# First head's first eight experts ahead of the rest, TensorE's order around them, and small moves at the start and in the gates, in a two-block transformer kernel on one core

## The reference

```python
for l in range(DEPTH):                       # 2
    h = rmsnorm(x, norm_mix_g[l])
    x = x + mixer_block(h, ...)              # mLSTM with 4 heads, windowed attention with 16 heads, gated
    h = rmsnorm(x, norm_mlp_g[l])
    x = x + sqrelu_mlp(h, w_up[l], w_down[l])
x = rmsnorm(x, final_norm_g)
```

```python
y = sum over heads and their 16 experts of
        softmax(best sums)[e] * gelu(x . expert_u[e]) * expert_v[e]
```

## Time and profile before

| | us |
|---|---|
| median of 3 runs | 1753.12 |
| lowest and highest | 1752.78, 1753.4 |
| the profiled execution's own time | 1752.94 |
| its span, first to last instruction | 1751.2 |

### The profile page before, as it was taken

One profiled execution on the slowest core, in us unless ns is written; L12 is line 12 of the kernel. 1 busy time (PEld: TensorE's weight loads), 2 busy tenths in 40 slices (PEclk: granted clock), 3 DMA queues, 4 the chain that ended last, 5 costly groups with the idle time before them and its releaser, 6 DMA issues.

```text
span 1751.2 us, 21314 instructions
## 1 busy us (share of the span) xinstructions
PE 1613.2 (92%) x8160; PEld 1183.5 (68%) x8160; DVE 1159.2 (66%) x2030; ACT 835.1 (48%) x1555; POOL 379.0 (22%) x374
## 2 busy tenths in 40 slices
PE   7999999999999999999999999799987788778786
PEld 6998998888898899888889998455522232222232
DVE  5757865666665776566675556788676767767654
ACT  4456635333455664533355545454444444444443
POOL 0100001000120000100050102565543444334440
PEclk9999999999999999999999999999999999999999
DMA  7444454555544355455544365999999999999996
GB/s 293 161 144 145 152 209 155 198 185 187 198 166 140 125 183 214 168 193 192 186 151 145 145 217 194 414 421 421 422 421 421 422 421 422 422 421 422 421 421 270
DMA packets 67206, 464.43 MB, mean 265 GB/s; under 512 B 7457, under 2 KB 9633, under 8 KB 11809
## 3 DMA queue, kind: packets, MB, share of 16 engines
q0 software_dynamic: 36864, 268.45, 36.9%
q1 hardware_dynamic: 29952, 194.29, 30.8%
q10 hardware_dynamic: 288, 0.33, 0.1%
HBM read 462.00 MB, written 1.05 MB: 264 GB/s over the span
## 4 chain that ended last, share of the span: by engine, by line
PE 65%; DMA 21%; DVE 6%; issue 4%; ACT 3%; POOL 0%; SPq 0%; POOLq 0%; ACTq 0%
PE acc L579 13%; PE acc L581 13%; PE acc L580 13%; DMA arena<-in_peer_uv,arena 10%; DMA row_w_lo<-in_peer_uv,arena 5%; PE att L604 5%; DMA row_w_hi<-in_peer_uv,arena 4%; PE acc L1718 4%; PE acc L1721 4%; PE acc L604 3%; PE att L605 3%; PE acc L605 1%; DVE w_lo L553 1%; DVE arena L2132 1%; PE att L904 1%
## 5 line engine op out<-in xcount | busy, mean ns | idle before, releaser
L553 DVE TENSOR_TENSOR w_lo<-arena,w_hi 128x2048 fp32r<-128x2048 f32 x171 | 391.7, 2300 | 172.8 <-ACT w_hi L546 172.5
L546 ACT CAST w_hi<-arena 128x2048 fp32r<-128x2048 f32 x175 | 333.6, 1907 | 121.8 <-PE acc L581 100.2
L1840 ACT ACTIVATE arena<-arena 128x1 f32<-128x1 f32 x256 | 51.9, 203 | 322.7 <-DVE arena L2132 139.5
L2132 DVE SCALAR_TENSOR_TENSOR arena<-arena 128x1024 f32<-128x1024 f32 x114 | 139.3, 1223 | 84.9 <-DMA arena<-in_peer_uv,arena 83.1
L579 PE MATMUL acc<-xa,w_hi 128*128 128x256 f32 x672 | 192.9, 287 | 0.0
L580 PE MATMUL acc<-xa,w_lo 128*128 128x256 f32 x672 | 190.8, 284 | 0.0
L581 PE MATMUL acc<-xa,w_hi 128*128 128x256 f32 x672 | 190.7, 284 | 0.0
L1718 PE MATMUL acc<-arena,gate_raw 128*128 128x512 f32 x226 | 128.1, 650 | 46.8 <-ACT gate_raw L1850 46.3
L2326 POOL DMA_INDIRECT arena<-in_peer_uv,arena x114 | 129.6, 1137 | 151.4 <-PE acc L1721 141.1
L604 PE MATMUL att<-xa,w_hi 128*128 128x512 f32 x384 | 136.0, 398 | 0.0
L579 PEld LDWEIGHTS acc<-xa,w_hi 128*128 128x128 f32 x672 | 129.2, 192 | 3.6 <-issue 3.0
(11 more groups left out here) (309 smaller groups left out, 3545.7 us busy)
## 6 DMA issues: line engine op xcount, KB each, us to landing
arena<-in_units SPq DMA_DIRECT2D x175, 1024.0 KB, 4.8
arena<-in_bias SPq DMA_DIRECT2D x1, 2048.0 KB, 9.3
arena<-in_peer_uv,arena POOLq DMA_INDIRECT x114
x_res<-in_x SPq DMA_DIRECT2D x2, 512.0 KB, 6.5
arena<-in_norm_mix_g SPq DMA_DIRECT2D x2, 512.0 KB, 6.9
arena<-in_units SPq DMA_DIRECT2D x2, 512.0 KB, 8.1
arena<-in_norm_mlp_g SPq DMA_DIRECT2D x2, 512.0 KB, 6.6
arena<-in_norm_g SPq DMA_DIRECT2D x2, 512.0 KB, 5.8
```

The costliest lines, as they stand in the source:

```text
L546: nc.scalar.copy(w_hi[:, s, :], raw[HOME[g]]).then_inc(S["hi_ready"], 1)
L553: nc.vector.tensor_tensor(w_lo[:, s, :], raw[HOME[g]], w_hi[:, s, :].bitcast(F32), ALU.subtract).then_inc(S["lo_ready"], 1)
L2132: nc.vector.scalar_tensor_tensor(row, row, 1.0, hn[:, n // SLOTS, :], ALU.mult, ALU.mult, accum_out=dots[:, n:n + 1]).then_inc(S["rows_use ...
```

## The change

It has four parts. (1) `first_experts()` on VectorE, ahead of tile 1's split: it takes the 8 best of each half's scores, the 64 sums of these, the 8 best sums and their experts, and writes the first 8 indices; the 8 best sums of 16 x 16 lie among these 64. GpSimd waits for it ahead of item 0 and for the whole routing of head 0 ahead of item 8. `route(0, 0)` leaves out what is done. (2) The order around it: on TensorE the second half of tile 0's queries runs through ahead of tile 1's transposes, which are cut in two around `rank_half(1)`; on ScalarE `first_take(1)` goes ahead of tile 1's copies; in unit mix 3, tile 0's transposes come one step earlier; on VectorE tile 0 is split whole ahead of the last sum; on GpSimd the iota goes ahead of tile 1's norm. (3) At the start, the first norm's weights are loaded on ScalarE's queue; unit 1 is rounded in two halves, and its remainder made half by VectorE, behind the norm of tile 1, and half by GpSimd. (4) `gate_columns` runs for heads 0 and 1 in the middle of unit aq 0, for heads 2 and 3 behind it.

```diff
@@ start
-            sp.dma_start(g_next, rows_of(A["norm_mix_g"][0:1, :])).then_inc(S["g_loaded"], mark("g_loaded", "mix", 16))
+            act.dma_start(g_next, A["norm_mix_g"][0:1, :].broadcast_to([P, D])).then_inc(S["g_first_loaded"], 16)
+        def second_hi(act, half):
+            cols = slice(half * UNIT // 2, (half + 1) * UNIT // 2)
+            if half == 0:
+                act.wait_ge(S[f"w_loaded{HOME[1]}"], at(f"w_loaded{HOME[1]}", 1))
+            nc.scalar.copy(w_hi[:, SLOT[1], cols], raw[HOME[1]][:, cols]).then_inc(S["first_hi" if half == 0 else "hi_ready"], 1)
+        def second_lo(eng, op, half):
+            cols = slice(half * UNIT // 2, (half + 1) * UNIT // 2)
+            if half == 0:
+                eng.wait_ge(S["first_hi"], 2)
+            else:
+                eng.wait_ge(S["hi_ready"], 2)
+                eng.wait_ge(S["lo_ready"], 1)
+            op(w_lo[:, SLOT[1], cols], raw[HOME[1]][:, cols], w_hi[:, SLOT[1], cols].bitcast(F32), ALU.subtract).then_inc(
+                S["first_lo" if half == 0 else "lo_ready"], 1)
@@ layer_act, l == 0
                 norm_act(act, "mix", 1)
-                split_hi(act, 1)
+                second_hi(act, 0)
+                second_hi(act, 1)
@@ layer_dve, l == 0
-                split_lo(dve, 1)
                 norm_dve(dve, "mix", 1, g_next)
+                second_lo(dve, nc.vector.tensor_tensor, 0)
@@ layer_pool
             norm_pool(pool, "mix", 1)
+            if l == 0:
+                second_lo(pool, nc.gpsimd.tensor_tensor, 1)
@@ layer_pe
+                    elif (l, u) == (0, 1):
+                        pe.wait_ge(S["first_lo"], 2)
+                        pe.wait_ge(S["lo_ready"], 2)
-                    within = {("gb", 3): turn_hm, ("aq", 1): gate_more_columns}.get((name, i), lambda: None)
+                    within = {("gb", 3): turn_hm, ("aq", 0): lambda: gate_columns((0, 1)), ("aq", 1): gate_more_columns}.get((name, i), lambda: None)
...
                 elif (name, i) == ("aq", 0):
-                    gate_columns()
+                    gate_columns((2, 3))
@@ by_tile
-                        half_t(b, s, xh, xl, t, k0[n_], first[n_], last[n_], range(3))
+                        half_t(b, s, xh, xl, t, k0[n_], first[n_], last[n_], range(2))
+                        if n_ == 1:
+                            earlier(t)
+                        half_t(b, s, xh, xl, t, k0[n_], first[n_], last[n_], range(2, 3))
@@ first_queries
                 queries_of(0, 1, range(4))
                 rank_half(0)
-                tile_pe(pe, "n2", 1)
                 queries_of(0, 1, range(4, 8))
-                queries_of(1, 0, range(2))
+                tile_pe(pe, "n2", 1, range(4))
                 rank_half(1)
-                queries_of(1, 0, range(2, 8))
+                tile_pe(pe, "n2", 1, range(4, 8))
+                queries_of(1, 0, range(8))
                 queries_of(1, 1, range(8))
@@ second_pe, mix 2
-                            lambda t: tile_pe(pe, "n2", 0) if t == 1 else None)
+                            earlier=lambda t: tile_pe(pe, "n2", 0) if t == 1 else None)
@@ second_act
             first_rank(0)
+            first_take(1)
             tile_act(act, xb_hi, "n2", 1)
-            first_take(1)
             first_rank(1)
@@ second_dve
+            def first_experts():
+                for i in range(2):
+                    scores_ = rank[0][:, i, :]
+                    dve.wait_ge(S["rank_ready"], at("rank_ready", (0, 0, i)))
+                    nc.vector.max(top_s[:, i, 0:8], scores_)...
+                    nc.vector.max_index(top_i[:, i, 0:8], top_s[:, i, 0:8], scores_)...
...
+                nc.vector.tensor_copy(expert[:, 0:8], f_expert).then_inc(S["expert_ready"], mark("expert_ready", "first"))
@@ peer_norm
-                tile_dve(dve, xb_hi, xb_lo, "n2", 0, [0])
+                tile_dve(dve, xb_hi, xb_lo, "n2", 0)
                 unit("mix", 3)
                 mix_add(1, 1)
-                tile_dve(dve, xb_hi, xb_lo, "n2", 0, [1])
                 norm_dve(dve, "n2", 1, g_peer)
+                first_experts()
                 tile_dve(dve, xb_hi, xb_lo, "n2", 1)
@@ second_pool
-            for t in range(TT):
-                norm_pool(pool, "n2", t)
+            norm_pool(pool, "n2", 0)
             nc.gpsimd.iota(iota_i, pattern=[[1, P_TOP]], base=0, channel_multiplier=0).then_inc(S["iota"], mark("iota", 0))
             pool.wait_ge(S["iota"], at("iota", 0))
             nc.gpsimd.tensor_copy(iota16, iota_i).then_inc(S["iota"], mark("iota", 1))
+            norm_pool(pool, "n2", 1)
...
             for n in range(ITEMS):
-                if n % P_TOP == 0:
+                if n == 0:
+                    pool.wait_ge(S["expert_ready"], at("expert_ready", "first"))
+                elif n % P_TOP == 0 or n == 8:
```

More of the change, by code:

```diff
@@ L82 @@
     "first_hi": "the rounded part of half of the first unit", "first_lo": "and the rest of it",
+    "g_first_loaded": "the first norm's weights are here",
     "first_loaded": "half of the first unit is here", "x_loaded_too": "the second tile of tokens is here",
@@ L442, in build @@
         wsum = area("ak", 1280, ALL_HEADS)
+        f_top = area("ak", 1296, 16).rearrange("p (i k) -> p i k", i=2)
+        f_cand = area("ak", 1312, 64).rearrange("p (a b) -> p a b", a=8)
+        f_best, f_pos = area("ak", 1376, 8), area("ak", 1384, 8).bitcast(U32)
+        f_pos_i = area("ak", 1392, 16).bitcast(U32).rearrange("p (i k) -> p i k", i=2)
+        f_pos_f = area("ak", 1408, 16).rearrange("p (i k) -> p i k", i=2)
+        f_pick = area("ak", 1424, 128).rearrange("p (i k a) -> p i k a", i=2, k=8)
+        f_both = area("ak", 1552, 16).rearrange("p (i k) -> p i k", i=2)
+        f_expert = area("ak", 1568, 8)
         ROW = 2 * D
@@ L468, in unit_dma @@
                 sp.wait_ge(S["lo_ready"], LAST_AT_HOME[g] + 1)
+            if LAST_AT_HOME[g] == 1:
+                sp.wait_ge(S["first_lo"], 2)
             s = HOME[g]
@@ L637, in half_t, with by_tile @@
             return m
-        def by_tile(pe, operands, ua, k0, first, last, tag, between=lambda t: None, normed=None, in_halves=False):
+        def by_tile(pe, operands, ua, k0, first, last, tag, between=lambda t: None, normed=None, in_halves=False,
+                    earlier=lambda t: None):
             for t in range(TT):
@@ L701, in norm_dve, with tile_pe @@
                     S["hn_ready"], mark("hn_ready", (tag, t, b)))
-        def tile_pe(pe, tag, t):
-            for k in range(KT):
+        def tile_pe(pe, tag, t, ks=range(KT)):
+            for k in ks:
                 if k % 4 == 0:
@@ L829, in gate_products, with gate_columns @@
                 m.then_inc(S["gate_done"], mark("gate_done"))
-            def gate_columns():
+            def gate_columns(heads):
                 pe.wait_ge(S["gate_m"], at("gate_m"))
-                for h in range(M_HEADS):
+                for h in heads:
                     nc.tensor.matmul(att[h // 2][:, (h % 2) * SEQ:(h % 2 + 1) * SEQ], ident[0:M_HEADS, h:h + 1].broadcast_to([M_HEADS, P]), g_M,
@@ L1390, in layer_dve @@
             if l == 0:
-                dve.wait_ge(S["g_loaded"], at("g_loaded", "mix", "start"))
+                dve.wait_ge(S["g_first_loaded"], 16)
                 norm_dve(dve, "mix", 0, g_next)
@@ L2069, in route @@
                 if part == 0 and g == 0:
-                    dve.wait_ge(S["iota"], at("iota", 1))
-                    for i in range(2):
-                        dve.wait_ge(S["rank_ready"], at("rank_ready", (0, 0, i)))
-                        top_first(t, h, halves[i:i + 1])
+                    for values, val, idx, i in halves:
+                        dve.wait_ge(S["routed"], at("routed", ("first8_at", i)))
+                        nc.vector.match_replace(values, val[:, 0:8], values, LOWEST).then_inc(
+                            S["routed"], mark("routed", ("top8_out", (t, h, i))))
                 elif part == 0:
@@ L2110, in route @@
                     dve.wait_ge(S["routed"], at("routed", ("expert_f", (t, h))))
-                    c = t * SLOTS + h * P_TOP
-                    nc.vector.tensor_copy(expert[:, c:c + P_TOP], expert_f).then_inc(
+                    c, known_ = t * SLOTS + h * P_TOP, 8 if g == 0 else 0
+                    nc.vector.tensor_copy(expert[:, c + known_:c + P_TOP], expert_f[:, known_:P_TOP]).then_inc(
                         S["expert_ready"], mark("expert_ready", (t, h)))
```

36 lines of the change are left out of this document (added).

## The result

The changed kernel took 1768.55 us (median of four runs, 1767.04 to 1769.5), the kernel before 1752.95 beside it: a ratio of 1.0088, 95% interval 1.0075 to 1.0102, so 15.6 us slower. The forecast was +0.4. The profiled execution took 1769.1, its span 1767.3, 16.1 more than before.

The account below looks back on a forecast made before the run. TensorE was taken to bound the kernel until about 1100 us, then the gather's DMA stream at 421 to 422 GB/s. Terms +1.1 - 1.5 + 0.8 = +0.4 us on 1752.94 gave 1753.3, as median 1753.5; range 1750.2 to 1755.8.

Parts of the forecast that it names:

- the clock's term: Behind TensorE's hole ahead of tile 1's queries: 3.2 us of work at half speed, 1.6 us; bounds 0 and 3.3.
- the slacks: Delay the gather's items can take: item 7 5.5 us, item 18 2.4 plus 2.4 of TensorE waits; gone at 4.8.
- experts ahead: First experts and the order around them: 1.1 us slower; 0.5 faster without the clock's fall, 2.8 slower with the long one.
- columns in three: Gate columns in shorter pieces keep TensorE's clock up behind them: 1.5 us faster, bounds 0 and 1.5.
- start: Unit 1's halves 1.0 us slower, norm weights on ScalarE's queue 0.2 faster: 0.8 slower; bounds 0.4 faster, 1.0 slower.
- The sum of first_experts(): VectorE's steps behind the second half's scores: 3.7 us in all, first numbers at 1084.2 instead of 1089.4.
- The iota moved ahead ... Both nothing.: On GpSimd ahead of the second norm: query unit 1's remainder starts sooner, ending before anyone wants it; no effect.
- The hole: TensorE idle 5.0 us ahead of tile 1's queries, waiting for tile_dve queued behind first_experts() on VectorE.
- Rival four: The hole costs double: clock at 1.2 GHz for 6.7 us of work, item 18 2.8 us late, 1755.2; chance 0.12.
- Row 0: First gathered row used 5.9 us later: 4.3 from the order and 1.6 from the clock.
- the 0.8 that was free: Ahead of row 0: of TensorE's 5.1 us delay, 0.8 is free before VectorE's remainder of query unit 3 ends.
- Item 7's slack of 5.5: In the gather: landing at 1115.7, less 4.65 us, less its issue's end at 1105.6; 0.4 us late after 5.9.

Follow-up runs that it names:

- hole_filled: experts_norm_first with 39 discarded matmuls (13 steps of three, 128 columns) put into TensorE's hole ahead of tile 1's queries: 1757.99 us, 1.0027 of the kernel before.
- hole_filled_full: As hole_filled, with 16 discarded steps instead of 13, which leave no pause: 1754.75 us, 1.0011 of the kernel before.
- experts_split_ahead: As experts_norm_first, with tile 1's split ahead of first_experts() on VectorE: 1751.5 us, 0.9991 of the kernel before.
- start_halves_vector: The kernel before with only unit 1's remainder in two halves, both on VectorE and nothing on GpSimd: 1752.96 us, 1.0000 of the kernel before.
- experts_norm_first: The kernel before with the experts' part alone, but GpSimd's iota and cast back behind both norms: 1760.83 us, 1.0043 of the kernel before.

## Why the prediction was wrong

Four steps failed: that moving the iota costs nothing (3.0 us), the clock's term (6.2 for 1.6), the columns (+1.4 for -1.5) and the start (+2.4 for +0.8); and the slacks held less than the sum gave them (2.3 us more). For the experts this closes: 3.0 + 4.6 + 2.3 = 9.9, and 11.05 - 1.1 = 9.95.

| term | forecast | alone on the chip |
|---|---|---|
| experts ahead | +1.1 | +11.05 |
| columns in three | -1.5 | +1.4 |
| start | +0.8 | +2.4 |
| sum | +0.4 | +14.8 (the whole: +15.6) |

- **The sum of first_experts().** Right: 3.6 us from the second half's MAX8 to the end of the cast (1089.12 to 1092.69) against 3.7, and the first numbers at 1084.06 where nothing disturbs it (1084.2 forecast).
- **"The iota moved ahead ... Both nothing."** This step failed. I asked when the remainder of query unit 1 is wanted, and not what runs on VectorE when it starts. It is a GpSimd instruction with two SBUF operands beside a VectorE one, the very pair that the prediction priced at the start. It cost 3 us. The Trainium skill, "SBUF — State Buffer", section "SBUF: two separate sides", says that whichever of the two starts first holds the ports for its whole instruction and the other is blocked. The trace agrees: a lead of 0.07 us decided over 4.3 (5.68 against 1.41).
- **The hole.** Right in size (5.05 us against 5.0) and in cause (tile_dve queued behind first_experts()).
- **The clock behind it.** The mechanism was right, the term mis-sized: 1.6 forecast, bounds 0 to 3.3, and 6.2 measured. It failed where I read how long the clock stays low from the products of whole rows (3.2 us, from 1100.8 to 1104.0). In tile 1's queries it stayed at 0.5 for all their 48 products of 128 columns (in hole_filled from the 22nd on), and came back 2.1 to 2.4 us (4.3 in hole_filled) after the 256-column products of head 1 had begun. Rival four had 6.7 us of low clock at most, and 1755.2.
- **Row 0.** 5.9 us late forecast. Without lock and clock (hole_filled_full) its product is at 1105.26, with 0.2 of drift: 4.3 late, the 4.3 of the order. In the changed kernel it is 18.55 - 5.0 = 13.55 late: 5.5 up to tile 1's queries for the order, 3.2 for the lock, and 4.9 (26.0 - 21.1) behind them, the clock's share less the 0.8 that was free.
- **The slacks.** 4.8 us forecast, about 2.5 found: 4.3 late gave +1.8, where the forecast's sum without the clock gave -0.5, and 13.55 gave 11.1. Item 7's slack of 5.5 failed first. It counts 4.65 us from the end of an issue to the row, but behind the gaps ahead of items 6 and 7 the stream moves 326 GB/s from 1112 to 1118 (419 before), and row 10's dot waits for its data until 1.8 us later than before. VectorE's timelines, hole_filled_full, then before:

```profile
1125.02 1.23 DVE L2197 SCALAR_TENSOR_TENSOR row_xa<-row_xa,arena 128x1024 f32<-128x1024 f32 x1 [2.05 <-DMA row_xa<-in_peer_uv,arena]
```
```profile
1123.23 1.23 DVE L2132 SCALAR_TENSOR_TENSOR row_xa<-row_xa,arena 128x1024 f32<-128x1024 f32 x1 [0.81 <-DMA row_xa<-in_peer_uv,arena]
```

TensorE does win back its waits up to row 11's product (1.7 late), but there stands a wait of 2.11 us, in before as well, and this time the clock reads 0.63 behind it (1134.5 to 1138.5, above), where in before it held. Row 12's product is 3.1 late, item 18 is issued 2.6 late, and the stream has 404 GB/s from 1140 to 1160 and not 420, which is another 0.8 us.

- **The columns.** The 1.5 us were read rightly in the earlier trace rows and put down wrongly. That the length of the piece brings the clock down isn't shown: hole_filled, experts_split_ahead and start_halves_vector have the whole piece at 70.9 to 71.2 as before has, and read 1.00 from 72.5 to 77.5. And I priced a piece ahead of aq 0's end at its own 1 us on TensorE, without asking who waits for aq 0's product. The chain of ScalarE and VectorE had no slack left: in layer 1 TensorE's products of keys and queries came just in time in before (515.40, with 0.04 us of idle ahead).
- **The start.** The halves at +1.0 were right (0.81 alone). The weights were forecast at -0.2 and cost 0.83: I counted the queue's issue of 0.42 and not what lands behind 0.5 MB (128 rows of 4 KB), the table of columns that GpSimd waits for. The two together crossed an order of arrival.
- **The range** (1750.2 to 1755.8) was built of cases in which each surprise stays single. Lock, hole and clock stood in one chain, and their costs added up (the hole is 5.2 us without the lock as well, in experts_norm_first).

## What to carry to other kernels

Before a call is moved ahead in a queue, look at what then starts at the same moment on the engine that shares its port, also when nobody is waiting for the moved call; a lead of a tenth of a microsecond can decide over four. Put new work behind what the busiest engine waits for: the same eight experts cost 8 us ahead of the split and gained 2 behind it, with the numbers ready 0.9 us later. A low clock is to be priced from products of the same shape: here a pause of 5 us cost half speed in all 48 products of 128 columns behind it, and not the 3.2 us of work that it lasted in front of whole rows.

## What the runs showed of the hardware

- The granted clock can stay at 0.5 for 12 us and more although TensorE never rests: 57 products in 12 us in the changed kernel, 48 of 128 columns and 9 of 256, all started 0.21 us apart; at 1.0 hole_filled_full ran 88 of the same two kinds in 10 us, 0.11 apart.
- In one trace a pause of 0.90 us between such products was followed by a fall; one of 0.58 behind products of 256 columns was not, nor was one of 0.58 in experts_split_ahead, where products of 128 columns stood ahead. What decides is open, the more so as hole_filled's times, 1754.14 to 1760.51, suggest that it did not fall in each run.
- The same instructions at the same time come with and without a fall from run to run (layer 0's columns: seven traces low and two at 1.00 among nine whose program is unchanged up to there). It is worth 1.3 us of 1753, so a gain of this size read in one trace needs more than one.
